# Attention outputs by query rows: probabilities loaded, values streamed, in a two-layer encoder kernel

## The chip, the cores and the metric

The kernel runs on one core of a Trainium2 chip. The metric is the device time of one launch in microseconds (us). The engines are called by their short names: PE is TensorE's matmul stream, PEld the loading of its stationary operand, DVE is VectorE, ACT is ScalarE, POOL is GpSimd, SP is SyncE, which here only issues transfers.

## The reference, cut to what matters

```python
for l in range(DEPTH):                       # DEPTH = 2, 1024 tokens, width 1024
    proj = jnp.einsum('btd,dp->btp', x, w_in[l])
    # four groups of four heads, head width 64
    o_a = chunked_relpos_attention(...)      # A: a band of 9 chunks of keys, a bias by distance
    o_b = sliding_window_gqa_sinks(...)      # B: a band of 2 chunks, a sink in the denominator
    o_c = differential_attention(...)        # C: two maps a head, o = P1 v - lam * P2 v
    o_d = dsa_attention(...)                 # D: only the 256 best keys of each query
    mix = jnp.concatenate([o_a, o_b, o_c, o_d], axis=-1)
    x = layer_norm(ALPHA * x + mix @ w_out[l], ...)
    hid = jnp.square(jax.nn.relu(x @ w_up[l]))
    x = layer_norm(ALPHA * x + hid @ w_down[l], ...)
```

Each head is softmax(scores + mask) times its values. Everything is fp32.

## The kernel before

One instruction stream per engine is written out by hand, twice (once a layer), and the engines wait for one another by counting semaphores. The order in each stream is the order of the Python code; nothing is reordered.

Large products split each fp32 operand into a high and a low part in the type fp32r and run three matmuls (hi·hi, hi·lo, lo·hi); the weights come in slabs of 128x512 through a ring of four, whose high parts are rounded by ACT (`weights_hi`, L1221) or POOL, and whose low parts are made by POOL.

**Attention.** The heads stand in the order C, A, B, D (`HEADS`). A C head has two maps, so there are 20 jobs a layer (`JOBS`). A job is worked in two halves of four query tiles (of 128 queries); a half is a run of steps, one per key tile (`STEPS`, 228 a layer). A step (job, kt, a, b) covers the key tile kt and the query tiles a to b-1, from one to four of them. For each step n the streams hold:

- PE: `score_t(n)` makes the transposed scores, keys down the partitions and queries along the row, up to 128x512, in bank 2 + n % 2. It ends in a matmul of 64 moved columns (L1033, L1029, a mask), in selection masks of 128 moved columns each (L1038, D), in a band mask (L1031, B), in the bias (L1026, A), or in the scores themselves.
- ACT: `exponent(n)` (L1357) writes `probT[n % 4]`, the probabilities, keys by queries.
- PE: `pv(n - 2)` (L1054) multiplies by the values. The values of a key tile, 128 keys by 64 columns and a column of ones, are the loaded operand, and up to 512 columns of `probT` move. The sum over key tiles stands transposed in PSUM, 65 rows by 512 queries, in bank 5 or 6; row 64 is the softmax denominator. Both operands are plain fp32, and such a matmul is two loads and two passes in the trace.
- ACT: `evacuate` (L1365) copies a finished half (a "turn", 40 a layer) to SBUF as `oe`. PE: `turn_out` (L1062) turns it back with four transposes into bank 4, five steps after the half ended. DVE: `take_output` (L1700 to L1711) divides by the denominator and writes `mix`.

Beside this, PE makes the next job's plain scores in pieces in all but the last four steps of a job (L978 to L984), from which DVE takes each query's largest value (`largest`, L1675). In the fourth step from the end of the job DVE closes them (`row_max`, L1687 and L1688, `mr`), and one step later PE turns `mr` (`turn_max`, L991, bank 4); ACT copies the row and sends it by DMA into the next job's operands (`mT`), for which that job's first `score_t` (L1016 or L1018) waits. Also beside it, the queries and keys of two heads at a time are turned through bank 4 in four steps (`turn_qk` L957, `take_turn`, `take_lo` L1595; `PAIR_AT`, `_pair_steps`), and sent to `stacks` by SP's DMAs. Everything that goes through bank 4 waits for its predecessor there (`MISC`, `misc_wait`): after a `turn_out`, for DVE's `o_out`. DVE does other work at the same step as `row_max` (`between`: the choice of keys for D, the bias tables).

**MLP.** The hidden width is worked in eight chunks; seven go through products q = 0 to 6 (L1161 to L1163, sums on DVE at L1891, operands by `operand_hi` and `operand_lo`), and the last one, `down_last` (L1187 to L1189), reads `last_hi` (ACT, L1441) and `last_lo` (DVE, `last_low`, L1868). Its first matmul waits for the first half of `last_lo` and for DVE's sums of q = 5 and q = 6.

Of the kernel before, what the change touches and what calls it, by code (L numbers as in the profile page):

```python
# [20 lines left out]
F32 = mybir.dt.float32  # L21
# [4 lines left out]
ALU = mybir.AluOpType  # L26
# [210 lines left out]

HEADS = [(kind, h) for kind in "CABD" for h in range(H)]
DV = HD

JOBS = [(hd, m) for hd in range(len(HEADS)) for m in range(2 if HEADS[hd][0] == "C" else 1)]
C_JOBS = 2 * H
# [48 lines left out]
FIRST_STEP = [min(n for n, z in enumerate(STEPS) if z[0] == j) for j in range(len(JOBS))] + [N_STEPS]  # L291
HALF_END = [n for n, z in enumerate(STEPS) if z[6]]
HALF_OF = {n: m for m, n in enumerate(HALF_END)}
LAG, TURN_LAG = 2, 5
LAST_STEPS = TURN_LAG + 1


def first_key(kind, i):
# [44 lines left out]
def max_turn_at(n):  # L343
    j, g, total = at_step(n)
    return j + 1 < len(JOBS) and g == total - 3
# [7 lines left out]
def _pair_steps():  # L353

    out = {}
    for p, (job, first) in PAIR_AT.items():
        n, j, last = FIRST_STEP[job] + first, 0, -2
        while j < 4:
            if n >= last + 2 and not max_turn_at(n) and not {n - TURN_LAG, n + 1 - TURN_LAG} & set(HALF_OF):
                assert n not in out  # L360
                out[n], last, j = (p, j), n, j + 1
            n += 1
    assert [out[n][0] for n in sorted(out)] == [p for p in PAIR_AT for _ in range(4)]
    return out
# [10 lines left out]
def _misc_turns():  # L375

    for j in range(4):
        yield "qk_lo", 4 * 0 + j
    yield "m_copied", 0
    for n in range(N_STEPS + LAST_STEPS):  # L380
        if pair_turn_at(n):
            p, j = pair_turn_at(n)
            yield "qk_lo", 4 * p + j
        if max_turn_at(n):
            yield "m_copied", at_step(n)[0] + 1
        if n - TURN_LAG in HALF_OF:
            yield "o_out", HALF_OF[n - TURN_LAG]


MISC = list(_misc_turns())  # L390
# [8 lines left out]
def build(nc, x_in, w_in, bias_in, sinks_in, lam_in, subln_in, w_out, ln_g, ln_b, w_up, w_down,  # L399
          ident_in, cs64_in, cs32_in, bmask_in, lam0_in, selc_in, bias_t_in, resid, out):  # L400
    with ExitStack() as ctx:
        sem_names = """w_hi w_hi_act w_lo w_used t_ready t_hi t_lo p_ready p_out i_rope i_turned
            i_ready i_relu i_acc roped qk_ready s_ready s_max thr_ready signed m_ready m_turned m_copied m_row st_ready p_done pv_done
            o_evac o_turned o_out es_ready ones_set bias_t_loaded bias_t_ready masks_ready pool_chain pool_roped mix_done o_ready o_sum x_loaded gb_loaded ln_done u_ready u_relu u_square h_sum
            u_hi u_lo d_ready d_sum halves misc_loaded bias_loaded chain lam_exp lam_dot
            k_candidate k_counted
            qk_hi qk_lo ik_hi ik_lo i_stacked""".split()
# [39 lines left out]
        bias_a = tensor("bias_a", [P, H, 2 * P], F32, r)  # L447
        farmask = tensor("farmask", [P, 3 * P], BF16, r + 8 * H * P)
        r += 8 * H * P + 6 * P
        oe = [tensor(f"oe{j}", [P, W], F32, r + 4 * W * j) for j in range(2)]  # L450
        r += 8 * W
        mT = tensor("mT", [P, P], F32R, r)
        es = tensor("es", [P, 2, TILES], F32, r + 4 * P)
# [95 lines left out]
        nm = tensor("nm", [P, 2, 2, TILES], F32)  # L549
        mr = tensor("mr", [P, 2, TILES], F32R)  # L550
        far = tensor("far", [P, H], F32)
        rinv = tensor("rinv", [P, 4], F32)


        halves = tensor("halves", [P, 3 * CHUNK], F32R)
# [241 lines left out]
        def tensor_layer(pe, l, S, prev):  # L797
# [243 lines left out]
            def values(kind, h, kt):  # L1041
                if kind == "D":
                    return raw_d[:, kt, D_V - D_Q:N_D + 1]
                return {"A": v_a, "B": v_b, "C": v_c}[kind][:, kt, h // 2 if kind == "B" else h, :]

            def pv(n):

                job, kt, a, b, half, fresh, end = STEPS[n]
                kind, h = HEADS[JOBS[job][0]]
                turn = 2 * job + half  # L1050
                pe.wait_ge(S["p_done"], n + 1)
                if turn >= 2:
                    pe.wait_ge(S["o_evac"], turn - 1)
                mm(ps[0:HD + 1, 5 + turn % 2, P * (a - 4 * half):P * (b - 4 * half)], values(kind, h, kt),  # L1054
                   probT[n % 4][:, 0:P * (b - a)], start=fresh, stop=end).then_inc(S["pv_done"], 1)

            def turn_out(turn):

                pe.wait_ge(S["o_evac"], turn + 1)
                misc_wait("o_out", turn)  # L1060
                for t in range(4):
                    last = nc.tensor.transpose(ps[:, 4, 65 * t:65 * t + 65], oe[turn % 2][0:65, P * t:P * t + P],  # L1062
                                               ident[0:65, 0:65])
                last.then_inc(S["o_turned"], 1)

            def first_pair(k):

# [13 lines left out]
            for n in range(N_STEPS + LAST_STEPS):  # L1081
                if n < N_STEPS:
                    score_t(n)
                if LAG <= n < N_STEPS + LAG:
                    pv(n - LAG)
                for p in pieces_at(n):
                    score(at_step(n)[0] + 1, p)
                if pair_turn_at(n):
                    turn_qk(*pair_turn_at(n))
                if max_turn_at(n):  # L1090
                    turn_max(at_step(n)[0] + 1)
                if n - TURN_LAG in HALF_OF:
                    turn_out(HALF_OF[n - TURN_LAG])


            pe.wait_ge(S["mix_done"], 1)
# [107 lines left out]
        def scalar_layer(act, l, S, prev):  # L1204
# [152 lines left out]
                nc.scalar.activation(probT[n % 4][:, 0:P * (b - a)], ps[:, 2 + n % 2, 0:P * (b - a)], ACT.Exp,  # L1357
                                     scale=SCALE[HEADS[JOBS[job][0]][0]]).then_inc(S["p_done"], 1)

            def evacuate(turn):  # L1360

                act.wait_ge(S["pv_done"], HALF_END[turn] + 1)
                if turn >= 2:
                    act.wait_ge(S["o_turned"], turn - 1)
                nc.scalar.activation(oe[turn % 2][0:65, :], ps[0:65, 5 + turn % 2, :], ACT.Copy).then_inc(S["o_evac"], 1)  # L1365

            take_max(0)
            for n in range(N_STEPS + LAST_STEPS):
                if n < N_STEPS:
                    exponent(n)  # L1370
                if pair_turn_at(n):
                    take_turn(*pair_turn_at(n))
                if max_turn_at(n):
                    take_max(at_step(n)[0] + 1)
                if n - LAG - 1 in HALF_OF:
                    evacuate(HALF_OF[n - LAG - 1])


            def load_norm(j):
# [58 lines left out]
            for half in range(2):  # L1438
                act.wait_ge(S["d_ready"], SUMS * (LAST - 1) + 4 * (4 + half) + 4)
                for f in range(4):  # L1440
                    nc.scalar.activation(last_hi[half][:, f], hidden[LAST % 2][:, f, W * half:W * half + W],  # L1441
                                         ACT.Copy).then_inc(S["u_hi"], 1)
                weights_hi(range(SLAB_LAST + RING * half, SLAB_LAST + RING * half + RING))
            weights_hi(range(SLAB_LAST + 2 * RING, N_SLABS))

            if l == DEPTH - 1:
                for t in range(TILES):
# [4 lines left out]
        def vector_layer(dve, l, S, finish_previous):  # L1452
# [237 lines left out]
            def take_output(turn):  # L1690

                job, half = divmod(turn, 2)
                hd, m = JOBS[job]
                kind, h = HEADS[hd]
                dve.wait_ge(S["o_turned"], turn + 1)
                o = ps[:, 4, 0:260].rearrange("p (t d) -> p t d", d=65)
                total = rinv[:].unsqueeze(2)
                if kind == "B":
                    dve.wait_ge(S["es_ready"], h + 1)
                    then(v_.tensor_tensor(total, o[:, :, HD:65], es[:, h % 2, 4 * half:4 * half + 4].unsqueeze(2), ALU.add))  # L1700
                    then(v_.reciprocal(rinv[:], rinv[:]))
                else:
                    then(v_.reciprocal(total, o[:, :, HD:65]))
                if m:
                    then(v_.tensor_scalar(rinv[:], rinv[:], nlam[:, 0:1], None, ALU.mult))
                at_ = mix[:, "ABCD".index(kind), 4 * half:4 * half + 4, HD * h:HD * h + HD]
                dst = other[:] if m else at_
                v_.tensor_tensor(dst, o[:, :, 0:HD], total.broadcast_to((P, 4, HD)), ALU.mult).then_inc(S["o_out"], 1)
                if m:
                    dve.wait_ge(S["o_out"], turn + 1)  # L1710
                    then(v_.tensor_tensor(at_, at_, other[:], ALU.add))  # L1711
# [63 lines left out]
            for n in range(N_STEPS + LAST_STEPS):  # L1775
                for p in pieces_at(n):
                    largest(at_step(n)[0] + 1, p)
                if pair_turn_at(n):
                    take_lo(*pair_turn_at(n))
                if n - TURN_LAG in HALF_OF:  # L1780
                    take_output(HALF_OF[n - TURN_LAG])
                if maxima_done_at(n):
                    if at_step(n)[0]:
                        row_max(at_step(n)[0] + 1)
                    between(at_step(n)[0])
# [124 lines left out]
            for c in range(LAST):  # L1910
                prepare(c)
                for q in range(N_PROD):
                    sum_product(c, q)
                    dve.wait_ge(S["d_sum"], SUMS * c + 4 * q + 4)
                    if q + PLACES < N_PROD:
                        operand_lo(c, q + PLACES)
                    elif c == LAST - 1 and q < N_PROD - 1:
                        last_low(q - 4)
            for t in range(4):
                add_common(t, 1)  # L1920
            for t in range(4, TILES):
                add_common(t, 0)
                add_common(t, 1)
# [101 lines left out]
```

## Time and profile before

| | |
|---|---|
| time before, median of 3 runs | 2896.27 us (2893.12 to 2899.35) |
| the profiled execution's own time | 2896.33 us |
| its span, first to last instruction | 2894.6 us |
| mean granted clock of PE | 0.976 |
| PE busy | 95% |
| PEld / DVE / POOL / ACT busy | 75% / 57% / 45% / 34% |

The profiled execution's own time stands 1.7 us above its span. A PE row's busy time includes the modelled end of the last matmul, so successive rows overlap; the distance from one start to the next is what a pass costs.

### The profile page before, as it was taken

The page shows a single profiled execution, that of the slowest core. Times are in us where ns is not written, and L with a number is a line of the kernel's source. Part 1 is how long each engine was busy: PE and PEld are TensorE (multiplying, and loading weights), DVE is VectorE, ACT ScalarE, POOL GpSimd, SP SyncE. Part 2 cuts the span into 40 slices and gives each one's busy share as a digit, 9 for nine tenths or more (in the row PEclk, how much of TensorE's full clock was granted, in tenths as well). Part 3 has the DMA queues.
Part 4 walks back from the last instruction along what each step waited for, and adds up shares of the span by engine and source line. Part 5 has one row for each costly group of instructions (what it writes and reads, how often), then busy time and mean ns, then how long its engine had stood idle before and what let it go on. Part 6 is the DMA issues. An engine that isn't in the chain of part 4 may idle for free. (4 is left out here: it accounts for less than half of the span.)

```text
span 2894.6 us, 36977 instructions
## 1 busy us (share of the span) xinstructions
PE 2756.7 (95%) x13160; PEld 2165.5 (75%) x13160; DVE 1640.7 (57%) x3369; ACT 979.6 (34%) x2011; POOL 1292.9 (45%) x1198
## 2 busy tenths in 40 slices
PE   8999999999899999999889999999999999999996
PEld 7788567768788888888677875676677888888875
DVE  3787776534444345544859867665254444355547
ACT  2575444442222212222226654443322222212231
POOL 5433600015566556666454354001155656556552
PEclk9999999999999999999999989999999999999998
DMA  4312234523301111110341122344233101111102
GB/s 148 81 48 62 54 64 93 121 99 95 103 18 59 58 59 59 56 50 19 94 132 52 42 68 45 71 104 116 99 91 106 44 19 59 59 59 59 55 26 92
DMA packets 98182, 205.16 MB, mean 71 GB/s; under 512 B 14032, under 2 KB 23056, under 8 KB 98000
## 3 DMA queue, kind: packets, MB, share of 16 engines
q1 hardware_dynamic: 88560, 175.37, 22.7%
q10 hardware_dynamic: 9440, 27.43, 2.6%
q8 instruction: 106, 1.74, 0.3%
q14 instruction: 76, 0.62, 0.1%
HBM read 139.93 MB, written 8.39 MB: 51 GB/s over the span
## 5 line engine op out<-in xcount | busy, mean ns | idle before, releaser
L787 POOL TENSOR_TENSOR wlo<-wraw,whi 128x512 fp32r<-128x512 f32 (+2 forms) x368 | 491.3, 1336 | 273.3 <-ACT whi L1221 251.5
L785 POOL CAST whi<-wraw 128x512 fp32r<-128x512 f32 (+2 forms) x272 | 178.1, 655 | 771.9 <-DMA wraw<-in_w_out 304.3
L1137 PE MATMUL ps<-xhi,whi 128*128 128x512 f32 x1024 | 409.2, 400 | 6.4 <-DVE xlo L1482 3.5
L1138 PE MATMUL ps<-xlo,whi 128*128 128x512 f32 x1024 | 408.5, 399 | 0.0
L1139 PE MATMUL ps<-xhi,wlo 128*128 128x512 f32 x1024 | 408.3, 399 | 0.0
L1891 DVE TENSOR_TENSOR common<-common,ps 128x512 f32<-128x512 f32 x104 | 69.6, 687 | 467.1 <-PE ps L1163 466.5
L1162 PE MATMUL ps<-wlo,op_hi 128*128 128x512 f32 x784 | 312.4, 398 | 0.0
L1161 PE MATMUL ps<-whi,op_hi 128*128 128x512 f32 x784 | 309.3, 395 | 0.0
L1357 ACT ACTIVATE probT<-ps 128x512 f32<-128x512 f32 (+2 forms) x456 | 205.4, 456 | 306.3 <-PE ps L1038 83.5
L1163 PE MATMUL ps<-whi,op_lo 128*128 128x512 f32 x784 | 307.5, 392 | 0.0
L1054 PE MATMUL ps<-probT,raw 128*65 128x512 f32 (+2 forms) x720 | 270.6, 458 | 0.0
L787 POOL TENSOR_TENSOR wlo<-down_raw,whi 128x512 fp32r<-128x512 f32 x168 | 226.1, 1349 | 98.6 <-ACT whi L1221 91.9
L831 PE MATMUL ps<-whi,xhi 128*128 128x512 f32 (+1 forms) x640 | 245.1, 383 | 8.3 <-DVE xlo L1482 5.1
L1400 ACT ACTIVATE hidden<-ps 128x512 f32<-128x512 f32 x128 | 75.9, 599 | 512.4 <-PE ps L1139 501.6
L1837 DVE TENSOR_TENSOR op_lo<-hidden,op_hi 128x512 fp32r<-128x512 f32 x196 | 204.1, 1086 | 76.1 <-ACT op_hi L1423 71.4
L832 PE MATMUL ps<-wlo,xhi 128*128 128x512 f32 (+1 forms) x640 | 243.1, 380 | 0.0
L833 PE MATMUL ps<-whi,xlo 128*128 128x512 f32 (+1 forms) x640 | 242.2, 379 | 0.0
L1137 PEld LDWEIGHTS ps<-xhi,whi 128*128 128x128 f32 x1024 | 194.6, 190 | 55.1 <-DVE xlo L1482 3.9
L1138 PEld LDWEIGHTS ps<-xlo,whi 128*128 128x128 f32 x1024 | 194.6, 190 | 47.3
L1139 PEld LDWEIGHTS ps<-xhi,wlo 128*128 128x128 f32 x1024 | 194.4, 190 | 47.6
L1891 DVE TENSOR_TENSOR x<-x,ps 128x512 f32<-128x512 f32 x248 | 169.6, 688 | 46.7 <-PE ps L1163 43.7
L1423 ACT ACTIVATE op_hi<-hidden 128x512 fp32r<-128x512 f32 x196 | 111.0, 621 | 247.4 <-PE ps L1163 202.4
(246 smaller groups left out, 5639.2 us busy)
## 6 DMA issues: line engine op xcount, KB each, us to landing
wraw<-in_w_up SPq DMA_DIRECT2D x144, 256.0 KB, 3.1
down_raw<-in_w_down SPq DMA_DIRECT2D x112, 256.0 KB, 3.7
wraw<-in_w_in SPq DMA_DIRECT2D x80, 256.0 KB, 2.7
stack<-q_part SPq DMA_DIRECT2D x72, 256.0 KB, 3.9
stack<-k_part SPq DMA_DIRECT2D x72, 256.0 KB, 4.9
wraw<-in_w_out SPq DMA_DIRECT2D x64, 256.0 KB, 2.7
wraw<-in_w_down SPq DMA_DIRECT2D x32, 256.0 KB, 2.7
stack<-q_part SPq DMA_DIRECT2D x48, 128.0 KB, 2.4
```

What stands on the lines that cost most here:

```text
L787: nc.gpsimd.tensor_tensor(wlo[j][:, 0:w], loaded, whi[j][:, 0:w].bitcast(F32), ALU.subtract).then_inc(S["w_lo"], 1)
L831: mm(o, a, whi[j][:, 0:w], start=(k == 0), stop=False)
L832: mm(o, a, wlo[j][:, 0:w], start=False, stop=False)
L833: last = mm(o, b, whi[j][:, 0:w], start=False, stop=(k == KT - 1))
L1054: mm(ps[0:HD + 1, 5 + turn % 2, P * (a - 4 * half):P * (b - 4 * half)], values(kind, h, kt), probT[n % 4][:, 0:P * (b - a)], start=fresh, ...
L1137: mm(ps[:, b, :], wh, xhi[:, k, tok], start=(k == 0), stop=False)
L1138: mm(ps[:, b, :], wh, xlo[:, k, tok], start=False, stop=False)
L1139: last = mm(ps[:, b, :], wl, xhi[:, k, tok], start=False, stop=(k == KT - 1))
L1161: mm(ps[:, bank, :], a, whi[j][:], start=(i == 0 and not more), stop=False, skip_group_check=more)
L1162: mm(ps[:, bank, :], a, wlo[j][:], start=False, stop=False, skip_group_check=more)
L1163: last = mm(ps[:, bank, :], b, whi[j][:], start=False, stop=(i == 1), skip_group_check=more)
L1891: ins = v_.tensor_tensor(xs, xs, p, ALU.add)
```

## The change

In `pv` the operands change places: for each of the step's query tiles, 128 columns of `probT` are loaded and the 65 columns of values and ones move. The output stands by query rows, 128 queries by 65, at column 65 times the tile in bank 5 or 6. `evacuate`, `turn_out`, `oe` and their semaphores go. `take_output` reads the banks directly, three steps after a half ends instead of five, and the first `pv` of a half waits for `o_out` of two turns before. Turns of queries and keys no longer keep clear of `turn_out`, so they follow one another at every second step. In the last MLP chunk ACT rounds two slabs instead of four between the two halves of `last_hi`, and DVE makes the second half of `last_lo` after the sum of q = 6 and four additions of `common`, no longer ahead of that sum.

```diff
-LAG, TURN_LAG = 2, 5
-LAST_STEPS = TURN_LAG + 1
+LAG, TAKE_LAG = 2, 3
+LAST_STEPS = TAKE_LAG + 1
...
-            if n >= last + 2 and not max_turn_at(n) and not {n - TURN_LAG, n + 1 - TURN_LAG} & set(HALF_OF):
+            if n >= last + 2 and not max_turn_at(n):
...
-        if n - TURN_LAG in HALF_OF:
-            yield "o_out", HALF_OF[n - TURN_LAG]
...
                 pe.wait_ge(S["p_done"], n + 1)
-                if turn >= 2:
-                    pe.wait_ge(S["o_evac"], turn - 1)
-                mm(ps[0:HD + 1, 5 + turn % 2, P * (a - 4 * half):P * (b - 4 * half)], values(kind, h, kt),
-                   probT[n % 4][:, 0:P * (b - a)], start=fresh, stop=end).then_inc(S["pv_done"], 1)
-
-            def turn_out(turn):
-
-                pe.wait_ge(S["o_evac"], turn + 1)
-                misc_wait("o_out", turn)
-                for t in range(4):
-                    last = nc.tensor.transpose(ps[:, 4, 65 * t:65 * t + 65], oe[turn % 2][0:65, P * t:P * t + P],
-                                               ident[0:65, 0:65])
-                last.then_inc(S["o_turned"], 1)
+                if fresh and turn >= 2:
+                    pe.wait_ge(S["o_out"], turn - 1)
+                for i in range(a, b):
+                    last = mm(ps[:, 5 + turn % 2, O_W * (i - 4 * half):O_W * (i - 4 * half) + O_W],
+                              probT[n % 4][:, P * (i - a):P * (i - a) + P], values(kind, h, kt),
+                              start=fresh and i == a, stop=end and i == b - 1)
+                last.then_inc(S["pv_done"], 1)
...
-            def evacuate(turn):
-
-                act.wait_ge(S["pv_done"], HALF_END[turn] + 1)
-                if turn >= 2:
-                    act.wait_ge(S["o_turned"], turn - 1)
-                nc.scalar.activation(oe[turn % 2][0:65, :], ps[0:65, 5 + turn % 2, :], ACT.Copy).then_inc(S["o_evac"], 1)
...
-                weights_hi(range(SLAB_LAST + RING * half, SLAB_LAST + RING * half + RING))
-            weights_hi(range(SLAB_LAST + 2 * RING, N_SLABS))
+                if half == 0:
+                    weights_hi(range(SLAB_LAST, SLAB_LAST + 2))
+            weights_hi(range(SLAB_LAST + 2, N_SLABS))
...
-                dve.wait_ge(S["o_turned"], turn + 1)
-                o = ps[:, 4, 0:260].rearrange("p (t d) -> p t d", d=65)
+                dve.wait_ge(S["pv_done"], HALF_END[turn] + 1)
+                o = ps[:, 5 + turn % 2, 0:4 * O_W].rearrange("p (t d) -> p t d", d=O_W)
...
-                if n - TURN_LAG in HALF_OF:
-                    take_output(HALF_OF[n - TURN_LAG])
+                if n - TAKE_LAG in HALF_OF:
+                    take_output(HALF_OF[n - TAKE_LAG])
...
-                    elif c == LAST - 1 and q < N_PROD - 1:
-                        last_low(q - 4)
+                    elif c == LAST - 1 and q == 4:
+                        last_low(0)
             for t in range(4):
                 add_common(t, 1)
+            last_low(1)
```

On PE, at the place in job 7 (a C head's second map) where a half is turned out and the maxima are turned, the instructions stood like this before. L1016 and L1033 are the scores and their mask, L1054 the product with the values (the shape is its output), L1062 the turning out, L991 the maxima.

```order
L1016 MATMUL ps<-stack_128,stack_129 128x512 [waits p_done_0]
L1033 MATMUL ps<-minus_big,halves 128x64
L1054 MATMUL ps<-probT_64,raw_72 65x512 [waits o_evac_0,p_done_0]
L1062 MATMUL ps<-ident_r,oe_58 128x65 [waits o_out_0,o_evac_0]
L1062 MATMUL ps<-ident_r,oe_58 128x65 x3
L1016 MATMUL ps<-stack_128,stack_129 128x384 [waits p_done_0]
L1033 MATMUL ps<-minus_big,halves 128x64
L1054 MATMUL ps<-probT_65,raw_72 65x512 [waits o_evac_0,p_done_0]
L991 MATMUL ps<-ident_r,mr 8x128 [waits o_out_0,m_ready_0]
```

The same place after the change, where the lines are L1014, L1031, L1053 and L989:

```order
L1053 MATMUL ps<-raw_70,probT_62 128x65 [waits p_done_0]
L1053 MATMUL ps<-raw_70,probT_62 128x65 x3
L1014 MATMUL ps<-stack_124,stack_125 128x384 [waits p_done_0]
L1031 MATMUL ps<-minus_big,halves 128x64
L1053 MATMUL ps<-raw_70,probT_63 128x65 [waits p_done_0]
L1053 MATMUL ps<-raw_70,probT_63 128x65 x3
L989 MATMUL ps<-ident_r,mr 8x128 [waits qk_lo_0,m_ready_0]
```

One instruction of 65x512 has become four of 128x65, the four L1062 between two steps are gone, and the maxima wait for the last turn of keys instead of DVE's output.

On DVE, the same job before, from the last turn of queries to the maxima; between the rows shown stand the L1675 of the pieces. L1703 to L1711 are `take_output`, L1687 and L1688 `row_max`.

```order
L1595 TENSOR_TENSOR q_part_75<-ps,q_part_74 128x512
L1703 RECIPROCAL rinv<-ps 128x4
L1705 TENSOR_SCALAR rinv<-rinv,nlam 128x4
L1708 TENSOR_TENSOR other<-ps,rinv 128x256
L1711 TENSOR_TENSOR mix<-mix,other 128x4x64
L1687 TENSOR_TENSOR nm<-nm 128x6
L1688 TENSOR_SCALAR mr<-nm 128x8
```

And after, where `take_output` is L1688 to L1696 and `row_max` L1669 and L1670:

```order
L1688 RECIPROCAL rinv<-ps 128x4
L1690 TENSOR_SCALAR rinv<-rinv,nlam 128x4
L1693 TENSOR_TENSOR other<-ps,rinv 128x256
L1696 TENSOR_TENSOR mix<-mix,other 128x4x64
L1577 TENSOR_TENSOR k_part_77<-ps,k_part_76 128x512
L1669 TENSOR_TENSOR nm<-nm 128x6
L1670 TENSOR_SCALAR mr<-nm 128x8
```

The output is no longer taken right ahead of the maxima: it stands two steps earlier, with the last pieces and a turn of keys behind it.

On DVE at the end of the seventh MLP chunk, before (L1891 are the sums of q = 5, 6 and what is before them, L1897 the additions of `common`):

```order
L1868 TENSOR_TENSOR last_lo<-hidden_94,last_hi_104 128x512 x4
L1891 TENSOR_TENSOR common<-common,ps 128x512 x4
L1868 TENSOR_TENSOR last_lo<-hidden_94,last_hi_105 128x512 x4
L1891 TENSOR_TENSOR x<-x,ps 128x512 x4
L1897 TENSOR_TENSOR x<-x,common 128x512 x12
```

And after:

```order
L1853 TENSOR_TENSOR last_lo<-hidden_92,last_hi_102 128x512 x4
L1876 TENSOR_TENSOR common<-common,ps 128x512 x4
L1876 TENSOR_TENSOR x<-x,ps 128x512 x4
L1882 TENSOR_TENSOR x<-x,common 128x512 x4
L1853 TENSOR_TENSOR last_lo<-hidden_92,last_hi_103 128x512 x4
L1882 TENSOR_TENSOR x<-x,common 128x512 x8
```

The second four of `last_lo` have moved behind the last sum and four of the twelve additions.

## Rows read from the trace of the kernel before

**Rows 1.** The page's busy times: busy us, share of the span, instructions
```profile
PE 2756.7 (95%) x13160; PEld 2165.5 (75%) x13160; DVE 1640.7 (57%) x3369; ACT 979.6 (34%) x2011; POOL 1292.9 (45%) x1198
```

**Rows 2.** Busy us (x count) of PE, PEld, DVE, ACT, POOL, PEclk, DMA: attention, C jobs
```profile
290.00:625.00 335.00, 314.04 (x1836) 219.32 (x1835) 209.48 (x666) 141.92 (x319) 59.33 (x61) 0.99 0.34 75
1722.00:2060.00 338.00, 317.36 (x1832) 221.33 (x1833) 209.20 (x663) 141.44 (x319) 59.09 (x61) 0.98 0.34 74
...
303.20:424.20 121.00, 109.80 (x566) 69.66 (x565) 91.33 (x278) 54.53 (x116) 39.50 (x43) 1.00 0.25 53
```

**Rows 3.** Timeline of PE: start us, us, instructions; one pv, one turn_out
```profile
562.28 1.02 PE L1054 MATMUL ps<-probT,raw_d 128*65 128x512 f32 x2
563.15 0.41 PE L1062 MATMUL ps<-ident_r,oe 65*128 65x65 f32 x4
563.36 0.42 PE L1018 MATMUL ps<-stack,stack 128*128 128x384 f32 x1
```

**Rows 4.** Timeline of PEld: five loads of 128 columns among short matmuls
```profile
568.43 0.19 PEld L981 LDWEIGHTS ps<-stack,stack 96*128 96x128 f32 x1
568.54 0.19 PEld L984 LDWEIGHTS ps<-minus_big,halves 128*128 128x128 f32 x1
568.65 0.19 PEld L980 LDWEIGHTS ps<-stack,stack 128*128 128x128 f32 x1
568.76 0.19 PEld L981 LDWEIGHTS ps<-stack,stack 96*128 96x128 f32 x1
```

**Rows 5.** Loads of 65 columns of values: ns min/median/max, first and last start
```profile
L1054 PEld LDWEIGHTS ps<-probT,raw x720: 134/139/250, 291.2 to 1984.1; 128*65 128x65 f32 x180
```

**Rows 6.** Waits: engine, line, waited for: us in total, times, longest
```profile
PE ps L991 <- DVE mr L1688: 11.7, 12, 1.9
PE ps L1187 <- DVE x L1891: 10.5, 2, 5.2
PE ps L1016 <- DMA stack<-mT: 6.8, 10, 2.3
PE ps L1062 <- ACT oe L1365: 5.0, 10, 0.7
PE ps L957 <- DVE mix L1708: 3.6, 6, 0.8
```

**Rows 7.** Timeline of all engines at the end of job 7's pieces
```profile
417.60 0.20 PEld L1054 LDWEIGHTS ps<-probT,raw 128*65 128x65 f32 x2
...
418.96 0.18 DVE L1703 RECIPROCAL rinv<-ps 128x4 f32<-128x4 f32 x1 [0.97 <-PE ps L1062]
...
419.02 1.05 PE L1054 MATMUL ps<-probT,raw 128*65 128x512 f32 x2
...
420.57 0.17 DVE L1688 TENSOR_SCALAR mr<-nm 128x8 fp32r<-128x8 f32 x1
420.79 0.08 PEld L991 LDWEIGHTS ps<-ident_r,mr 128*8 128x8 f32 x1 [1.60 <-DVE mr L1688]
```

**Rows 8.** Timeline of ACT, DVE and PE before the last MLP chunk
```profile
1381.63 0.63 ACT L1221 ACTIVATE whi<-wraw 128x512 fp32r<-128x512 f32 x1 [2.16 <-PE ps L1163]
1382.16 2.17 ACT L1441 ACTIVATE last_hi<-hidden 128x512 fp32r<-128x512 f32 x4
...
1375.83 2.47 DVE L1891 TENSOR_TENSOR common<-common,ps 128x512 f32<-128x512 f32 x4
1382.88 3.17 DVE L1868 TENSOR_TENSOR last_lo<-hidden,last_hi 128x512 fp32r<-128x512 f32 x4 [4.58 <-ACT last_hi L1441]
1385.97 2.47 DVE L1891 TENSOR_TENSOR x<-x,ps 128x512 f32<-128x512 f32 x4
...
1386.79 0.76 PE L1187 MATMUL ps<-whi,last_hi 128*128 128x512 f32 x1 [5.25 <-DVE x L1891]
```

**Rows 9.** Busy time by stretch: right after that stall, columns as in Rows 2
```profile
1386.25:1389.70 3.45, 2.91 (x7) 2.36 (x8) 3.42 (x7) 0.00 (x0) 0.00 (x0) 0.51 0.02 5
```

More of the change, by code:

```diff
@@ L239 @@
 DV = HD
+O_W = DV + 1
 JOBS = [(hd, m) for hd in range(len(HEADS)) for m in range(2 if HEADS[hd][0] == "C" else 1)]
@@ L403, in build @@
             i_ready i_relu i_acc roped qk_ready s_ready s_max thr_ready signed m_ready m_turned m_copied m_row st_ready p_done pv_done
-            o_evac o_turned o_out es_ready ones_set bias_t_loaded bias_t_ready masks_ready pool_chain pool_roped mix_done o_ready o_sum x_loaded gb_loaded ln_done u_ready u_relu u_square h_sum
+            o_out es_ready ones_set bias_t_loaded bias_t_ready masks_ready pool_chain pool_roped mix_done o_ready o_sum x_loaded gb_loaded ln_done u_ready u_relu u_square h_sum
             u_hi u_lo d_ready d_sum halves misc_loaded bias_loaded chain lam_exp lam_dot
@@ L449, in build @@
         r += 8 * H * P + 6 * P
-        oe = [tensor(f"oe{j}", [P, W], F32, r + 4 * W * j) for j in range(2)]
         r += 8 * W
@@ L551, in build @@
         far = tensor("far", [P, H], F32)
-        rinv = tensor("rinv", [P, 4], F32)
+        rinv = tensor("rinv", [P, 2, 4], F32)
         halves = tensor("halves", [P, 3 * CHUNK], F32R)
@@ L1091, in tensor_layer @@
                     turn_max(at_step(n)[0] + 1)
-                if n - TURN_LAG in HALF_OF:
-                    turn_out(HALF_OF[n - TURN_LAG])
             pe.wait_ge(S["mix_done"], 1)
@@ L1374, in scalar_layer @@
                     take_max(at_step(n)[0] + 1)
-                if n - LAG - 1 in HALF_OF:
-                    evacuate(HALF_OF[n - LAG - 1])
             def load_norm(j):
@@ L1694, in take_output @@
                 kind, h = HEADS[hd]
-                dve.wait_ge(S["o_turned"], turn + 1)
-                o = ps[:, 4, 0:260].rearrange("p (t d) -> p t d", d=65)
-                total = rinv[:].unsqueeze(2)
+                dve.wait_ge(S["pv_done"], HALF_END[turn] + 1)
+                o = ps[:, 5 + turn % 2, 0:4 * O_W].rearrange("p (t d) -> p t d", d=O_W)
+                if turn >= 2:
+                    dve.wait_ge(S["o_out"], turn - 1)
+                inv = rinv[:, turn % 2]
+                total = inv.unsqueeze(2)
                 if kind == "B":
                     dve.wait_ge(S["es_ready"], h + 1)
-                    then(v_.tensor_tensor(total, o[:, :, HD:65], es[:, h % 2, 4 * half:4 * half + 4].unsqueeze(2), ALU.add))
-                    then(v_.reciprocal(rinv[:], rinv[:]))
+                    then(v_.tensor_tensor(total, o[:, :, HD:O_W], es[:, h % 2, 4 * half:4 * half + 4].unsqueeze(2), ALU.add))
+                    then(v_.reciprocal(inv, inv))
                 else:
-                    then(v_.reciprocal(total, o[:, :, HD:65]))
+                    then(v_.reciprocal(total, o[:, :, HD:O_W]))
                 if m:
-                    then(v_.tensor_scalar(rinv[:], rinv[:], nlam[:, 0:1], None, ALU.mult))
+                    then(v_.tensor_scalar(inv, inv, nlam[:, 0:1], None, ALU.mult))
                 at_ = mix[:, "ABCD".index(kind), 4 * half:4 * half + 4, HD * h:HD * h + HD]
@@ L1779, in vector_layer @@
                     take_lo(*pair_turn_at(n))
-                if n - TURN_LAG in HALF_OF:
-                    take_output(HALF_OF[n - TURN_LAG])
+                if n - TAKE_LAG in HALF_OF:
+                    take_output(HALF_OF[n - TAKE_LAG])
                 if maxima_done_at(n):
```

## The prediction

> **What bounds the kernel now.** I read the page's busy times first: PE is busy 95% of the span, and no other engine is over 75% [rows 1]. So a microsecond counts only if PE's stream gets shorter or PE waits less. Then the busy time by stage: attention takes 335 and 338 us in the two layers, with a granted clock of 0.99 and 0.98, so nearly always its upper level, 2.4 GHz [rows 2]. Then the list of waits, for what PE stands idle for [rows 6], and the timeline for what a pass costs. The reader should see two things. PE is the chain almost everywhere. And among its idle times are some that exist only for what this change takes out or moves: the wait for `oe`, the wait for DVE's `mix` in bank 4, most of the wait for `mr`, and the wait ahead of the last MLP chunk.
>
> **PE's stream, the product with the values.** The steps are counted from the code: a layer has 84 of four query tiles, 36 of three, 60 of two and 48 of one, in all 612 tiles, so 1,224 in two layers. Before, a step of 512 columns is two passes from 562.28 to 563.15, 0.87 us, so 0.435 a pass [rows 3]. The load of 65 columns is hidden behind them. Per tile that is 2 x 0.109 = 0.218 us, and 266 us in both layers.
>
> After, a tile is two loads of 128 columns and two passes of 65. A pass of 65 columns at the same rate is 0.435 x 65 / 512 = 0.055 us. The trace has no fp32 load of 128 columns outside of transposes. The nearest rows are loads of 128 columns in fp32r, of the same four bytes, among matmuls of 64 and 128 columns: they start at 568.43, 568.54, 568.65 and 568.76, so one in 0.11 us [rows 4]. The load of 65 columns of fp32 stands beside them: one lasts 0.139 us [rows 5], and two in a row take 0.20 from the first's start to the second's end [rows 7], so the second starts 0.06 after the first, half of 0.11 for half of the columns. So loads go by columns in both types, and I take 0.11 us a load, with the pass hidden behind the next load. That makes 2,448 passes x 0.11 = 269 us, **+3 us**. The bounds: 0.06 us, at which the turned-out halves go (four transposes, each with a load of 128 columns, in 0.21 to 0.24 us, rows 3), gives -119 us; load and pass one after the other, 0.165 us, gives +138. The value is nearest to rows 4, since those are no transposes.
>
> **At the edges of a step.** Before, the last matmul of the scores hides the load of 65 columns (0.055). Now it has to hide one of 0.11. Where the scores end in 64 or 128 moved columns it is too short by 0.05. From the code these are 148 steps a layer (64 of C, 24 of A, 12 of B, 48 of D): 296 x 0.053 = **+16 us**. Behind a step the next load is already in the 0.11 of the last pass; where that is a transpose (L991, L957; 26 a layer) it is shorter by 0.05, **-3 us**.
>
> **What goes from PE's stream.** 80 turned-out halves at 0.21 to 0.28 us each (0.21 between the recorded starts; a start is recorded up to 0.03 early there) [rows 3]: 80 x 0.25 = **-20 us**. So the stream itself comes out at 3 + 16 - 3 - 20 = -4 us: next to nothing. ACT loses 80 copies; it is busy 142 us of an attention stage of 335 [rows 2], so that is worth nothing by itself.
>
> **What goes from PE's waits.** The wait for `oe`: 5.0 us [rows 6], all of it, since DVE and not PE reads next. The wait for `mix` in bank 4: 3.6 us [rows 6], all of it. The wait for `mr`: 11.7 us in 12 waits [rows 6]. Job 7 shows why [rows 7]: DVE waits 0.97 us for L1062, takes the output (418.96 to 420.3), and only then closes the maxima at 420.57 to 420.74, while PE, done with its pass at about 419.9, stands until 420.79. After the change `take_output` waits for a `pv` of a step earlier and stands two steps earlier, so the maxima are closed at about 418.5. I count all 11.7 as gone, and what DVE then owes elsewhere as a term of its own. A job's first score waits for the row of maxima, 6.8 us in 10 waits with the longest 2.3 [rows 6]: that one is job 6's, in either layer, behind SP's transfers of stacked queries and keys, and the other eight are 0.3 each. Those transfers now are issued three steps earlier. That is 2 x 2.0, **-4 us**, and I am least sure of it.
>
> Against it: DVE is busy 91.3 of 121 us in C jobs 1 to 7, and its waits there are for PE [rows 2]. In the second maps (jobs 1, 3, 5, 7) `take_output`, 1.4 us with its four instructions [rows 7], moves from behind the pieces in among them, and in four pair turns two more of DVE's subtractions do. Where DVE has no slack PE now waits for `nm` in a score piece. At most this is 1.4 x 4 jobs x 2 layers = 11 us; at least nothing. I take **+5 us**. The first `pv` of a half queues behind it scores, pieces and turns, but it waits for an output that DVE took four or more steps earlier: no cost. Sum of the waits: -5.0 - 3.6 - 11.7 - 4 + 5 = **-19 us**.
>
> **The last MLP chunk.** PE stands 5.25 us ahead of L1187 [rows 8], 10.5 in two layers [rows 6]. ACT rounded four slabs ahead of the second half of `last_hi` (the last at 1381.63), DVE waited 4.58 us for that, then made four of `last_lo` (3.17 us), and only then summed q = 6, for which PE waited [rows 8]. Now DVE goes from 1378.5 straight to q = 6, whose sums end 0.7 us after PE's last matmul of it, and PE needs them one bank at a time, so nothing is left of the wait. What is late next: ACT's second half of `last_hi` stands ahead of the third slab. Slabs are 2.8 us apart (2.16 idle and 0.63 busy, rows 8), so the second was rounded at 1376.0 and the third at 1378.8; the 2.17 us of `last_hi` end at about 1378.8, just in time. After the stall the granted clock was 0.51, so the lower level, 1.2 GHz, and the seven matmuls there took 2.91 us [rows 9], half of which is lost: 1.4 us a layer. So 2 x (5.25 + 1.4) = **-13 us**.
>
> **Sum.** -4 - 19 - 13 = -36 against the profiled time 2896.33, which is the median of the runs (2896.27) within 0.1: 2860. The waits for turned queries and keys (in A job 10 a turn stood behind DVE's `between`, and no longer does) may give 2 us more, and the list leaves out what lies under a modelled matmul end (1.05 us for two passes of 0.435, rows 7, so 0.18 each in 28 waits, 5 us). I take half of these 7 and predict **2857 us**, with 2842 to 2874 for this case by itself.
>
> **Rivals.** *A: only the MLP part is left.* DVE or the clock takes the gain in attention back. DVE at its bound (+11 instead of +5), no gain at `mT`, and some falls of the granted clock, since the array now streams 0.055 of each 0.11 us in a product. For it: after DVE's long jobs PE already waits for `nm`, and the clock fell after stalls [rows 9]. Against it: in the steps that are left PE streams scores in full, so the mean stays well above half. A fall of 3.4 us at half clock costs 1.7; six of them 10 us. Time: 2857 + 6 + 4 + 10 = 2877.
>
> *B: slower, load and pass don't overlap.* In `pv` each load would wait for the pass ahead of it. The price is 0.055 x 2,448 = 135 us, so 2857 + 135 = 2992; the point from which it decides is 39 / 2448 = 0.016, a pass of 0.126 us instead of 0.11. Against it: two loads of 65 columns start 0.06 apart while the first pass lasts 0.43 [rows 5, 7], and rows 4 hold their 0.11 with matmuls of 64 columns among them. For it: no row has an fp32 pass shorter than its load. The Trainium skill, "TensorE: Matmul & The Clock Gate", "What overlaps and what doesn't", says that a load overlaps a running matmul only when it goes to another group of rows, which none here does; by that rule this rival is the forecast. The trace disagrees with it at the loads of rows 7.
>
> *C: faster, loads go quicker than 0.11.* For it: the transposes' 0.06 in rows 3. At 0.08, half way down, 2,448 x 0.03 = 73 us less, 2784. Against it: rows 4, which are not bound by anything else. The same page gives, under "Back-to-back issue gap", some 81 ns for a pair of load and matmul of 128 columns, sustained, which is this rival; rows 4 have 110 ns.
>
> **How the numbers follow.** Chances: my forecast 0.60, A 0.20, B 0.10, C 0.10. A time that is right 8 times in 10 leaves B and C out: the forecast's range and A's together, 2834 to 2887. A measurement of this kernel tells 0.2% (5.8 us) from nothing. Faster by over 0.2% are the forecast, C and nearly all of A: 0.86. Within 0.2%: the end of A and a pass of about 0.125, 0.05. Slower: 0.09, B.
>
> **What would show it.** In the profile after: loads of `probT` 0.11 us apart, with 65-column matmuls 0.11 apart; no wait of PE for `oe` or `mix`; the wait for `mr` under 3 us; the waits of L976 to L979 for `nm` larger by up to 5 us a layer; each attention stage 10 to 13 us shorter; no gap ahead of the last chunk's first matmul, and the granted clock full there. The prediction is wrong if loads of `probT` stand more than 0.12 apart, if the granted clock is below 0.95 in attention, or if a new wait on `o_out` or `qk_lo` shows at the first `pv` of a half or at L955.

## The result and the profile after

| | before | after |
|---|---|---|
| median of the runs | 2897.81 us (2893.12 to 2899.54) | 2998.42 us (2953.07 to 3026.49) |
| ratio, 95% interval | | 1.0237 [1.0159, 1.0316] |
| profiled execution's own time | 2896.33 us | 3018.2 us |
| span | 2894.6 us | 3016.4 us |
| mean granted clock | 0.976 | 0.918 |

The changed kernel is slower by 2.4%, within 1.6 to 3.2%, where 2857 us and a gain were forecast. Its four times scatter widely, with mean clocks of 0.941, 0.932, 0.918 and 0.915 from the shortest to the longest. The ratio rests on the two faster ones of them, 2953.07 and 2978.64 us, while the median is of all four and the profile of one of the longer ones. Every one of the four is longer than every run before.

The page of the changed kernel, busy times and the row of the clock, which answer to [rows 1]:

```profile
PE 2914.8 (97%) x14376; PEld 2472.2 (82%) x14376; DVE 1658.7 (55%) x3369; ACT 943.2 (31%) x1931; POOL 1290.7 (43%) x1198
...
PEclk9998557999999999999999975589999999999998
```

PE has 1,216 instructions more and is busy 158 us longer. The clock row shows where: three slices at the start of attention in each layer at 5 to 7 tenths. Cut at the places where the trace's clock record changes, with the columns of [rows 2]:

```profile
265.00:275.60 10.60, 9.19 (x72) 8.49 (x70) 5.82 (x22) 5.98 (x13) 2.84 (x3) 1.00 0.55 128
275.60:490.60 215.00, 212.72 (x888) 201.71 (x889) 106.98 (x320) 52.34 (x110) 62.22 (x63) 0.50 0.20 43
490.60:560.00 69.40, 69.23 (x559) 67.90 (x558) 47.45 (x161) 27.30 (x61) 0.94 (x1) 1.00 0.41 85
1770.60:1985.60 215.00, 212.99 (x889) 201.84 (x889) 107.14 (x320) 52.71 (x110) 62.25 (x64) 0.50 0.20 44
```

The last columns are the granted clock, the DMA share and GB/s. In each layer the clock stands at the lower level, 1.2 GHz, for 215.0 us, and PE is busy in 212.7 and 213.0 of them. This fall is not new. The same cut in the kernel before:

```profile
276.90:294.00 17.10, 14.40 (x42) 9.93 (x42) 14.68 (x49) 3.48 (x8) 16.07 (x14) 0.50 0.71 158
294.00:500.00 206.00, 191.40 (x1067) 132.31 (x1065) 147.54 (x449) 91.35 (x199) 48.12 (x50) 1.00 0.30 65
```

Before, the clock fell at the same place, among the score pieces of the first job, some 12 us ahead of the first steps, and came back after 17.1 us. In both kernels PE had just waited for the stacked keys:

```profile
274.42 0.30 PE L978 MATMUL ps<-stack,stack 96*128 96x128 f32 x1 [1.31 <-DMA stack<-k_part]
273.47 0.30 PE L976 MATMUL ps<-stack,stack 96*128 96x128 f32 x1 [1.31 <-DMA stack<-k_part]
```

The first line is from before, the second from after. After the change the clock does not come back until the C heads are nearly through: the first scores of an A head stand at 500.2, 9.6 us behind the return. (The expectation of run 3 below puts the return in the A heads; that is misread.) Taken one by one the passes with the values show both levels. The load's and the pass's rows of L1053, first in the half-clock stretch, then behind it:

```profile
L1053 PE MATMUL ps<-raw,probT x518: 309/417/456, 290.7 to 488.8; 128*128 128x65 f32 x173
L1053 PEld LDWEIGHTS ps<-raw,probT x517: 329/333/333, 290.8 to 488.7; 128*128 128x128 f32 x173
...
L1053 PEld LDWEIGHTS ps<-raw,probT x412: 187/192/353, 491.9 to 621.8; 128*128 128x128 f32 x138
L1053 PE MATMUL ps<-raw,probT x412: 218/275/417, 492.1 to 621.9; 128*128 128x65 f32 x138
```

And the timeline of PEld, groups of such loads at half and at full clock:

```profile
399.79 1.40 PEld L1053 LDWEIGHTS ps<-raw,probT 128*128 128x128 f32 x6
...
522.30 0.86 PEld L1053 LDWEIGHTS ps<-raw,probT 128*128 128x128 f32 x7
```

A row's length less one load, over the count less one, is the distance: (1.40 - 0.33) / 5 = 0.214 us at 1.2 GHz, (0.86 - 0.19) / 6 = 0.112 us at 2.4 GHz. The second is the 0.11 of the forecast. The first says that the load itself takes nearly twice as long at the lower level.

The waits, against [rows 6]:

```profile
PE ps L989 <- DVE mr L1670: 6.1, 6, 1.9
...
PE ps L1016 <- DMA stack<-mT: 5.5, 8, 0.9
PE ps L955 <- DVE k_part L1577: 5.3, 2, 2.6
```

The waits for `oe` and `mix` are gone, and no new one stands in their place that could pay for 100 us. Last, the start of the last MLP chunk on PE, against [rows 8]:

```profile
1451.85 0.39 PE L1153 MATMUL ps<-whi,op_lo 128*128 128x512 f32 x1
1452.08 0.39 PE L1177 MATMUL ps<-whi,last_hi 128*128 128x512 f32 x1
1452.32 0.40 PE L1178 MATMUL ps<-wlo,last_hi 128*128 128x512 f32 x1
```

The gap of 5.25 us is closed: 0.23 us from start to start. So the MLP's term looks right, and one thing that was no term of the sum costs more than all of them.

### The profile page after: what moved, and what is told of

It reads as the page before. It is cut to its first block, busy times and chain, and to the rows that moved or that the text cites. A ratio compares the mean times of both kernels' runs of the same rounds, so it can differ in the third digit from the quotient of the medians.

```text
span 3016.4 us, 38867 instructions
## 1 busy us (share of the span) xinstructions
PE 2914.8 (97%) x14376; PEld 2472.2 (82%) x14376; DVE 1658.7 (55%) x3369; ACT 943.2 (31%) x1931; POOL 1290.7 (43%) x1198
## 4 chain that ended last, share of the span: by engine, by line
PE 89%; DVE 7%; DMA 1%; SPq 1%; ACT 1%; issue 0%; ACTq 0%; POOL 0%; DVEq 0%
PE ps L1053 12%; PE ps L1127 8%; PE ps L1128 8%; PE ps L1129 8%; PE ps L1152 6%; PE ps L1151 6%; PE ps L1153 6%; PE ps L829 4%; PE ps L830 4%; PE ps L831 4%; PE ps L1014 2%; PE ps L976 2%; PE ps L1100 2%; PE ps L1102 2%; PE ps L1101 2%; PE ps L978 2%
## 5 line engine op out<-in xcount | busy, mean ns | idle before, releaser
L1053 PE MATMUL ps<-raw,probT 128*128 128x65 f32 x1872 | 375.8, 352 | 0.0
L1053 PEld LDWEIGHTS ps<-raw,probT 128*128 128x128 f32 x1872 | 360.4, 272 | 10.9
```

Of the source, the lines that this page charges most:

```text
L1053: last = mm(ps[:, 5 + turn % 2, O_W * (i - 4 * half):O_W * (i - 4 * half) + O_W], probT[n % 4][:, P * (i - a):P * (i - a) + P], values(kin ...
```

## The experiments

**The theory:** A fall of the clock, which stands behind a wait of PE in either kernel, lasts for as long as PE's work is mostly passes of 65 columns behind loads of 128. By the forecast's 0.055 us the pass fills only half of the load's 0.11 us. At the lower level both take about twice as long (a load 0.214 us; for a matmul of 512 columns [rows 9] have 0.42 us, the rows above 0.23), so it fills half of it there too. **Rivals:** the lower clock is only what this kernel gets for its denser stream from the start, stall or not; or something else in the change (outputs 65 apart in a bank, reading the bank on DVE, the MLP part) makes the time.

The first four ran on one chip, with the kernel before at 2895.64 us.

**1. The MLP part alone**, on the kernel before:

```diff
-                weights_hi(range(SLAB_LAST + RING * half, SLAB_LAST + RING * half + RING))
-            weights_hi(range(SLAB_LAST + 2 * RING, N_SLABS))
+                if half == 0:
+                    weights_hi(range(SLAB_LAST, SLAB_LAST + 2))
+            weights_hi(range(SLAB_LAST + 2, N_SLABS))
...
-                    elif c == LAST - 1 and q < N_PROD - 1:
-                        last_low(q - 4)
+                    elif c == LAST - 1 and q == 4:
+                        last_low(0)
...
+            last_low(1)
```

> The kernel before with the last MLP chunk's rounding order alone changed; attention is as before. By the prediction's term (2 x (5.25 wait + 1.4 at half clock)) it takes 13 us less, about 2884, ratio 0.9954, with no gap ahead of the last chunk's first matmul. If that part were what slowed the changed kernel, the ratio would be over 1.

Measured: 2880.88 us (2879.37 to 2885.44), ratio 0.9949 [0.9936, 0.9962], that is -14.8 us for a forecast of -13. The stretch behind the old gap, with the columns of [rows 9]:

```profile
1382.50:1386.00 3.50, 3.50 (x17) 2.82 (x16) 3.45 (x5) 0.63 (x1) 2.00 (x2) 1.00 0.28 80
```

PE starts 17 instructions in 3.5 us where it had 7, at the upper level. This term stands, and the loss is all in attention.

**2. 128 moved columns instead of 65 in every pass.** The 63 columns more are those that lie beside the head's values in SBUF; what comes of them in PSUM is read by nobody. Outputs stand 128 apart.

```diff
-                return {"A": v_a, "B": v_b, "C": v_c}[kind][:, kt, h // 2 if kind == "B" else h, :]
...
+                if kind in O_WIDE:
+                    c = min(c, end - P)
+                    return block_[:, kt, c:c + P]
...
-                    last = mm(ps[:, 5 + turn % 2, O_W * (i - 4 * half):O_W * (i - 4 * half) + O_W],
+                    last = mm(ps[:, 5 + turn % 2, O_STEP * (i - 4 * half):O_STEP * (i - 4 * half) + (P if kind in O_WIDE else O_W)],
```

> The changed kernel, but each product with the values moves 128 columns in place of 65 (the other 63 are neighbouring columns, whose results nobody reads; outputs stand 128 columns apart). Loads, their number and all waits stay. Theory 1 (clock): the changed kernel's profile has half clock from 276 to 491 us and again from 1771 to 1986 us, because the array streams only half of the time in these passes, at either clock, since a load takes twice as long at the lower one; a pass of 128 columns takes 0.11 us, just what its load takes, so it costs nothing and fills the array: granted clock 0.97 or more, 2845 to 2875 us. Theory 2 (the loads by themselves, or the new waits, are what costs): no gain from more columns, 2950 to 3030 us or more, since the array has more to do. In between, with some cold stretches: 2880 to 2940.

Measured: 2855.43 us (2850.74 to 2857.18), ratio 0.9857 [0.9843, 0.9871]: 143 us less than the changed kernel's median, by columns whose results are thrown away. Attention's first stretches, cut at the clock record, and a group of loads:

```profile
277.40:297.90 20.50, 17.54 (x61) 14.61 (x61) 14.80 (x51) 4.51 (x10) 19.20 (x18) 0.50 0.58 131
297.90:495.90 198.00, 190.00 (x1493) 181.88 (x1491) 152.04 (x453) 79.75 (x175) 44.87 (x47) 1.00 0.33 70
```

```profile
416.23 0.97 PEld L1064 LDWEIGHTS ps<-raw,probT 128*128 128x128 f32 x8
```

The fall is there and lasts 20.5 us, where it lasted 17.1 before the change. A pass of 128 columns costs (0.97 - 0.19) / 7 = 0.111 us, the same as one of 65. From the first pass to the last of the C, A and B heads, by the rows of this line and of L1053 in the changed kernel, it is 250.0 and 248.4 us in the two layers here, and 332.1 and 332.0 there: 82.1 and 83.6, together 165.7 us between them, where the two spans differ by 162.4. The whole loss lies in that stretch; the D heads take 72.2 to 72.5 us in both.

**3. 128 columns in the C heads only** (`O_WIDE = 'C'`), and **5. in the A, B and D heads only** (`'ABD'`, on another chip, the kernel before at 2897.57 us). Both have the outputs 128 apart.

> As the kernel with 128 moved columns, but in the C heads alone; A, B and D heads move 65. In the changed kernel's profile the half clock covers the C heads and the beginning of the A heads, and ends by itself in the A heads. Theory 1 with the cold stretch made in the C stage: as with all heads wide, 2845 to 2880 us. If the A, B or D heads can lose the clock by themselves too: 2880 to 2950, with falls after the C stage. Theory 2: 2950 to 3030.

> The complement of the kernel that is wide in C alone: 128 moved columns in the A, B and D heads, 65 in the C heads. Theory 1 with the C stage as the place where a low clock stays: long stretches at half clock from 276 us on and from about 1770 on, as in the changed kernel or longer stretches of it, 2940 to 3030 us. If any filling of half the passes sufficed: 2850 to 2880.

Measured: C only 2859.20 us (2848.84 to 2861.94), ratio 0.9866 [0.9847, 0.9885]; A, B and D only 3024.41 us (2979.58 to 3032.74), ratio 1.0361 [1.0300, 1.0422]. In run 5 the clock is low again through the C heads:

```profile
276.60:512.10 235.50, 232.70 (x978) 221.71 (x978) 111.53 (x337) 56.37 (x120) 61.91 (x62) 0.50 0.20 42
```

So it was enough to widen the passes of the C heads. And where an output stands in its bank is no cause: run 5 has the spacing of run 2 and is as slow as the changed kernel (2979.58 to 3032.74 us for 2953.07 to 3026.49).

**4. The change with 65 columns, and 30 long matmuls ahead of each layer's steps**, whose results nobody reads. They are to end the low clock before the first pass with the values.

```diff
+WARM = 30
...
+            for _ in range(WARM):
+                mm(ps[:, 6, :], stacks[SLOT[0]][1][0:96, 0:P], stacks[SLOT[0]][0][0:96, 0:W], start=True, stop=True)
```

> The changed kernel with 65 columns everywhere, and 30 extra matmuls of 512 columns into a free bank ahead of each layer's first attention step, whose result nobody reads. They take 30 x 0.23 to 0.43 = 7 to 13 us a layer and fill the array at the place where the clock is low before the steps. Theory 1a (the state at the entry lasts: a low clock isn't given back, a full one isn't taken in these steps): full clock through the C heads, 2870 to 2885 us. Theory 1b (the steps themselves take the clock away again, whatever it was at the entry): again long stretches at half clock, 2970 to 3040 us. Theory 2: 2970 or more with the clock full.

Measured: 2938.50 us (2916.06 to 2970.14), ratio 1.0120 [1.0075, 1.0166]. That lies in neither range of the expectation. The extra matmuls themselves take 9.7 and 9.0 us in the two layers. By the clock record of the one profiled execution (2923.32 us), layer 1 in two rows and then layer 2:

```profile
293.50:498.30 204.80, 197.21 (x1545) 188.82 (x1544) 150.59 (x453) 83.04 (x183) 47.04 (x49) 1.00 0.32 68
498.30:515.40 17.10, 17.10 (x83) 16.44 (x83) 6.62 (x27) 3.94 (x14) 0.00 (x0) 0.50 0.41 88
1713.50:1768.10 54.60, 52.41 (x395) 49.01 (x393) 38.43 (x110) 21.74 (x48) 46.65 (x49) 1.00 0.17 36
1768.10:1884.20 116.10, 116.10 (x493) 111.34 (x492) 55.76 (x165) 28.48 (x60) 0.94 (x1) 0.50 0.20 42
```

Layer 1 speaks against the rival that the denser stream gets the lower clock from the start. There the passes of 65 columns run for 204.8 us, through all C and A heads, at the full clock and as fast as those of 128 do (7.5 instructions a us, as in run 2). Layer 2 limits this: the clock falls at 1768.1, within the C heads, and then stays low for 116.1 us, in which PE does not idle at all. What made it fall there is open: PE's two waits in the 8 us ahead of it, timeline of PE,

```profile
1761.61 0.49 PE L1015 MATMUL ps<-stack,stack 97*128 97x512 f32 x1 [0.16 <-DMA stack<-mT]
1765.62 0.50 PE L977 MATMUL ps<-stack,stack 96*128 96x512 f32 x1 [0.62 <-DVE nm L1660]
```

are short, and one of 0.59 us for the same `nm` at 344.89 in layer 1 did nothing of the kind. So it is not excluded that such a stream can lose the clock with hardly a wait; that it needs a stall is not shown. The other executions have mean clocks of 0.961, 0.946 and 0.941 for 0.959 here, so two of them lost more of it, at places that no profile shows.

The row from 498.30 limits the theory in another way. It lies where the A heads end and the B heads begin, behind the longest wait of this stretch,

```profile
497.05 0.66 PE L956 MATMUL ps<-ident_r,raw_d 128*128 128x128 f32 x4 [2.63 <-DVE k_part L1580]
```

and the passes behind it move 65 columns too, but in B heads, and there the clock came back after 17.1 us. The same wait in the changed kernel, of 2.6 us, is followed by only 3.4 us at half clock (from 575.9). That a fall lasts for the rest of the stage is seen in the C heads alone.

**6. Run 2 with the outputs taken five steps after a half's end** (`TAKE_LAG` 5 instead of 3; same chip as run 5):

> 128 moved columns in all heads, but DVE takes a half's output five steps after it ends, as before the change, and not three. The prediction's step says that the earlier place frees PE from the wait for mr, 11.7 us in the kernel before; the wide kernel still has 9.6 us in 10 waits there. If the earlier place is worth nothing: 2850 to 2860, the same. If it is what saves part of it: 2860 to 2866.

Measured: 2874.45 us (2872.57 to 2876.10), ratio 0.9922 [0.9910, 0.9935], 19 us more than run 2 and beyond the expectation. Waits of PE:

```profile
PE ps L991 <- DVE mr L1681: 12.0, 12, 1.9
PE ps L1064 <- DVE mix L1705: 7.1, 12, 1.1
...
PE ps L1064 <- DVE other L1705: 5.4, 6, 1.0
```

The wait for `mr` is back at its old 12, and the first pass of a half now waits 12.5 us for the bank: together 15 us of the 19.

**7. Run 2 with two fillers of 512 columns behind each score piece of jobs 0 and 1** (same chip; results unread), to shorten the 20 us at half clock that are left:

> 128 moved columns in all heads, and behind each of the score pieces of jobs 0 and 1 two extra matmuls of 512 columns into a free bank, whose result nobody reads, where PE waits for DVE and the clock falls (from 277 us on, 20 us at half clock in the first layer and 17 in the second). If the clock stays full there and the steps that follow gain: 3 to 8 us less than with 128 columns alone, 2847 to 2853. If the fillers delay the pieces instead: 2858 to 2870.

Measured: 2863.31 us (2856.34 to 2880.88), ratio 0.9887 [0.9860, 0.9914]. Three of the six executions lie at 2856.3 to 2856.8 with clocks of 0.988 and 0.989, three at 2869.8 to 2880.9. The profiled one, at 2875.95, has the low stretch unshortened, 23.9 us; the others have no profile. The gain that was expected did not come: it is no better than run 2.

**8. Run 2 with `TAKE_LAG` 2, and 9. run 2 once more**, on one chip, the kernel before at 2894.52 us:

> All passes with 128 moved columns, TAKE_LAG 2 in place of 3. The run with TAKE_LAG 5 was 19 us slower than the one with 3, and showed new waits of fresh PV passes on the bank. If that goes on in the same direction, the takes come earlier still and this gives 2845 to 2853 us (ratio 0.982 to 0.985). Rival: the take now comes before DVE is through with the mix, so that turns and mr waits on PE grow: 2858 to 2866 us. Same as with 3 (2850 to 2860) if the bank is free in time with either.

> The kernel with 128 moved columns in all passes and TAKE_LAG 3 once more, on the same chip as the run with TAKE_LAG 2, so that the two can be compared. 2850 to 2860 us, ratio 0.986 within 0.002, granted clock 0.98, and no half clock stretch longer than 25 us.

Measured: 2857.15 us (2854.38 to 2857.78) and 2857.12 us (2856.21 to 2859.46), ratios 0.9867 [0.9849, 0.9885] and 0.9868 [0.9850, 0.9885]. Taking the outputs two or three steps after a half's end makes no difference, so the expectation of more gain falls: with two the list has 13.3 us for `mr` in 16 waits, where run 9 has 10.5 in 10. Run 9 repeats run 2. Runs 2, 3, 8 and 9 all beat the kernel before by 1.3 to 1.4%, and cannot be told from one another.

## Why the prediction was wrong

**The step that failed** is in rival A: "in the steps that are left PE streams scores in full, so the mean stays well above half", and with it "a fall of 3.4 us at half clock costs 1.7; six of them 10 us". The forecast saw that the array streams 0.055 of each 0.11 us in a product, and priced what that does to the clock with falls that end by themselves. The trace before had the fall that mattered, 17.1 us ahead of the steps in each layer; [rows 2] begin at 290.00 and leave out most of it, and it was not in the sum. After the change this one fall lasts 215.0 us. Its price is the 82.1 and 83.6 us between the changed kernel and run 2, and not 1.7. Shown: what decides is the moved columns of the C heads' passes. With 128 the clock comes back after 17 to 21 us (runs 2 and 3), with 65 a low clock stayed to the end of the C heads or nearly so in all five layers in which there was one during their steps (two of the changed kernel, two of run 5, layer 2 of run 4), and at the full clock passes of 65 run at full pace (layer 1 of run 4). Not shown: why the lower clock holds on; no run has a width between 65 and 128. The forecast named "granted clock is below 0.95 in attention" as a sign of its being wrong, and that is the sign that came.

The time lies nearest to that of rival B, 2992 us, but B's mechanism is not there: load and pass overlap, 0.112 us apart at full clock. The Trainium skill, "TensorE: Matmul & The Clock Gate", "What overlaps and what doesn't", which has no overlap here, is against these rows at either level: no wait of a load for its pass shows. Rival C's load of 0.08 us did not come either.

A check on size, from two executions: a mean clock of 0.918 over 3016.4 us is 495 us of half clock (2 x 0.082 x 3016.4), and run 2's 0.980 over 2854.0 us is 114. Their own times differ by 3018.2 - 2855.8 = 162 us, so 0.42 us for each us of half clock. The shortest run of the change has a clock of 0.941, so 348 us of half clock; at 0.42 that is 2956, and it took 2953. So the scatter between its runs fits this same cost, though only one of them has a profile.

**The other terms**, read from runs 1, 2 and 9, where the clock is not in the way:

- The sum: 2857 was forecast, 2855.43 and 2857.12 measured with the same instructions but wider passes. Attention got 8.0 and 13.3 us shorter in run 2, from the first pass with the values to the last, where -4 - 19 was forecast for both layers. That the totals meet so closely is partly luck, as the waits show.
- PE's stream: 0.11 us a load was right (0.112, and 0.111 with 128 columns). Edges, transposes and what goes were not measured one by one.
- Waits: -19 forecast. Three that grew or shrank and weren't in [rows 6], in the kernel before:

```profile
PE ps L957 <- DVE q_part L1595: 6.1, 4, 2.4
...
PE ps L978 <- DVE nm L1675: 4.7, 5, 1.8
...
PE ps L980 <- DVE nm L1675: 2.9, 4, 0.9
PE ps L957 <- DVE k_part L1595: 2.1, 4, 0.8
```

  and the list of run 2:

```profile
PE ps L991 <- DVE mr L1681: 9.6, 10, 1.9
...
PE ps L1018 <- DMA stack<-mT: 5.2, 7, 0.8
PE ps L957 <- DVE k_part L1588: 5.2, 2, 2.6
...
PE ps L978 <- DVE nm L1668: 2.2, 5, 0.6
...
PE ps L1016 <- DMA stack<-mT: 1.5, 2, 0.8
PE ps L957 <- DVE q_part L1588: 1.0, 2, 0.5
```

  `oe` and `mix` went in full (-8.6). "All 11.7" of `mr` was wrong: -2.1. It was right for jobs 3, 5 and 7, where the output had been taken right ahead of the maxima (at job 7, L991 is loaded at 417.12 with no wait). But these are only 6 of the 12 waits, some 0.72 us each; the wait in job 1 grew from 0.73 to 1.47 us, and the other ones stayed or are new. The term of +5 for DVE had the wrong sign: `nm` went from 7.6 to 2.2, -5.4. `mT` gave -0.3 instead of -4: job 6's wait of 2.3 is gone, but the scores of L1018 now wait 5.2 instead of 0.2. `q_part` and `k_part` together gave -2.0, where half of "may give 2 us more" was counted. The sum of these is -18.4 for -19, right by luck: the errors cancel.
- The last MLP chunk: -14.8 for -13.
- The earlier take (three steps for five): worth 19 us by run 6, in the forecast only as parts of the `mr` and `mT` terms.

## What to carry to other kernels

When operands change places so that a 128-column load carries a short pass, look in the trace of before for every stretch at half clock and ask whether the new instruction mix can end it, not only what the mix costs at full clock; one low stretch ahead of it may then cost the whole phase, here 82 us a layer. If the pass is hidden behind its load, widen it to the width of the load: here the extra columns cost nothing measurable and brought 143 us. Long matmuls ahead of the phase did not do instead: run 4 kept the clock in one layer and lost it in the other. And when terms of waits are summed, list every wait of the stage in both directions, since a moved step gives back here what it takes there.

## What the runs showed of the hardware

- An fp32 load of 128 columns is issued every 0.112 us at 2.4 GHz and every 0.214 us at 1.2 GHz; a recorded load lasts 192 and 333 ns. Passes of 65 and of 128 columns behind it cost the same, 0.112 and 0.111 us.
- The granted clock can stay at 0.50 while PE never idles: 116.1 us busy of 116.1 in run 4. The Trainium skill, "TensorE: Matmul & The Clock Gate", "HAM oscillation — how this bites in real kernels", ties the low clock to PE's idle gaps between bursts of work. The trace agrees in part: the fall at 275.60 stands behind a wait of 1.31 us. It does not agree on what keeps the clock low.
- The same stream of 65-column passes ran 204.8 us at 1.00 and 215.0 us at 0.50. In layer 1 of run 4 and in the changed kernel the level that it began with lasted; in layer 2 of run 4 it changed midway, behind no wait over 0.62 us.
- From the long low stretches the clock returned near the end of the C heads. In four of five that was 11 to 14 us after PE had begun the score pieces of the first A head (478.0 and 490.6 in layer 1 of the changed kernel), in the fifth, layer 1 of run 5, 34 us after (477.9 and 512.1). Whether these pieces bring it back, and what let the clock fall at 1768.1 in run 4, was not settled.
